# A fifteenth expert input behind the scatter, VectorE's work interleaved block by block there, and 64-wide products in alternation

## What is computed

```python
# first block: retention state of the context, per head (8 heads, keys 64 wide, values 128 wide)
w = jnp.exp(lg[:, None] * (l - 1 - jnp.arange(l)))
s = jnp.einsum('bhld,bhle,hl->bhde', k, v, w)          # one forward, one backward

# second block, RWKV-7 (8 heads of 64)
w_log = -jax.nn.softplus(-(w0 + jnp.tanh(zw) @ w_up)) - 0.5
a = jax.nn.sigmoid(a0 + za @ a_up)
g = jax.nn.sigmoid(zg) @ g_up
# per step: S = S * w_t + (S @ -kk_t) b_t + v_t k_t;  y_t = S @ r_t

# second block, PEER
act = jax.nn.gelu(jnp.einsum('tkd,td->tk', u_emb[eb], tb), approximate=False) * gb
out = jnp.einsum('tk,tkd->td', act, v_emb[eb])
```

## Time and profile before

| | us |
|---|---|
| median of 3 runs | 1875.15 (1874.86 to 1876.91) |
| the profiled execution | 1877.81 |
| its span, first to last instruction | 1876.0 |
| TensorE busy | 1740.2 (93%) |
| VectorE busy | 1184.8 (63%) |
| ScalarE busy | 814.3 (43%) |
| mean granted clock of TensorE | 0.956 |

### The profile page before, as it was taken

How to read it: one execution, slowest core, us unless ns; L and a number is a source line. 1 busy time by engine, 2 the same in 40 slices (tenths; PEclk the granted TensorE clock), 3 DMA queues, 4 the chain that set the end, 5 groups by cost and what they waited for, 6 DMA issues and landing times.

```text
span 1876.0 us, 31040 instructions
## 1 busy us (share of the span) xinstructions
PE 1740.2 (93%) x11808; PEld 1579.8 (84%) x11808; DVE 1184.8 (63%) x2140; ACT 814.3 (43%) x1223; POOL 110.6 (6%) x124
## 2 busy tenths in 40 slices
PE   8799889899998988788889988799999999999997
PEld 1799868899998976687688877699999999999997
DVE  0656556677745657742357999666666666666665
ACT  2334346466544465311241289244444444444443
POOL 0000000022200000150003400000000000000000
PEclk9899899899999989887699999999999999999999
DMA  8576313445553521100133310355555555555553
GB/s 320 210 268 228 111 45 137 177 167 184 183 185 126 187 92 68 68 1 1 68 113 135 131 43 31 135 182 193 185 181 196 182 183 196 180 184 195 180 186 116
DMA packets 38527, 279.13 MB, mean 149 GB/s; under 512 B 4400, under 2 KB 4528, under 8 KB 5040
## 3 DMA queue, kind: packets, MB, share of 16 engines
q1 hardware_dynamic: 35136, 254.82, 38.3%
q0 software_dynamic: 2304, 16.78, 2.3%
q10 hardware_dynamic: 1008, 6.41, 0.9%
HBM read 276.94 MB, written 1.05 MB: 148 GB/s over the span
## 4 chain that ended last, share of the span: by engine, by line
PE 82%; DVE 10%; ACT 4%; issue 2%; DMA 1%; DVEq 0%; SPq 0%; POOL 0%; ACTq 0%; POOLq 0%
PE ps L443 81%; DVE piece L1479 1%; DMA ring<-in_stream 1%; ACT piece L1062 1%; DVE arena L1793 1%; DVE pconst_sb L2126 1%; DVE cols L2126 0%; DVE late L2126 0%; DVE arena L1536 0%; DVE arena L1559 0%; DVE arena L1885 0%; ACT arena L1096 0%; DVEq L2126 0%; DVE late L2143 0%; ACT arena L1166 0%
## 5 line engine op out<-in xcount | busy, mean ns | idle before, releaser
L443 PEld LDWEIGHTS ps<-h_r,piece 128*128 128x128 f32 x5664 | 708.6, 195 | 37.0 <-issue 25.4
L443 PE MATMUL ps<-h_r,piece 128*128 128x256 f32 x5664 | 716.3, 286 | 21.6 <-DVE h_r L1540 9.5
L1479 DVE TENSOR_TENSOR piece<-ring,piece 128x1024 fp32r<-128x1024 f32 x434 | 535.0, 1239 | 307.4 <-ACT piece L1062 305.9
L1062 ACT ACTIVATE piece<-ring 128x1024 fp32r<-128x1024 f32 x432 | 453.3, 1056 | 408.9 <-PE ps L443 395.8
L443 PE MATMUL ps<-piece,late_r 128*128 128x512 f32 x1536 | 374.4, 393 | 9.9 <-DVE late_r L2148 9.9
L443 PEld LDWEIGHTS ps<-piece,late_r 128*128 128x128 f32 x1536 | 282.5, 190 | 66.5 <-issue 10.8
L443 PE MATMUL ps<-arena 64*128 64x256 f32 (+7 forms) x712 | 126.4, 386 | 34.1 <-DVE arena L1826 8.8
L2143 DVE TENSOR_TENSOR late<-late,arena 128x256 f32<-128x256 f32 x114 | 72.7, 638 | 119.6 <-ACT late L1441 119.6
L443 PEld LDWEIGHTS ps<-arena 128*128 128x128 f32 (+3 forms) x712 | 94.9, 210 | 60.6 <-issue 20.5
L1441 ACT ACTIVATE late<-ps 128x256 f32<-128x256 f32 x114 | 43.9, 385 | 202.7 <-PE ps L443 202.7
L443 PE MATMUL ps<-arena,ring 128*128 128x256 f32 x480 | 110.5, 379 | 1.6 <-DVE arena L1536 1.6
(11 more groups left out here) (309 smaller groups left out, 1813.6 us busy)
## 6 DMA issues: line engine op xcount, KB each, us to landing
ring<-in_stream SPq DMA_DIRECT2D x240, 1024.0 KB, 4.9
arena<-in_mod POOLq DMA_DIRECT2D x16, 1024.0 KB, 5.6
arena<-in_const ACTq DMA_DIRECT2D x1, 2256.0 KB, 8.4
arena<-in_const ACTq DMA_DIRECT2D x1, 2000.0 KB, 9.6
xres<-in_xT SPq DMA_DIRECT2D x1, 1024.0 KB, 10.6
arena<-in_xT SPq DMA_DIRECT2D x1, 1024.0 KB, 12.6
arena<-in_subk ACTq DMA_DIRECT2D x1, 1024.0 KB, 4.8
out<-arena SPq DMA_DIRECT2D x2, 512.0 KB, 2.7
```

What stands on the lines that cost most here:

```text
L443: mm_last[0] = nc.tensor.matmul(*args, **kw)
L1062: A(piece[:, 0, c % 3], ring[:, p % RING, s], ACT.Copy).then_inc(S["hi_ready"], 1)
L1479: TT(piece[:, 1, c % 3], ring[:, p % RING, s], piece[:, 0, c % 3].bitcast(F32), ALU.subtract).then_inc(S["lo_ready"], 1)
```

## The change

- **A fifteenth early input.** EARLY is 15. The fifteenth up block is not done in the scatter but right behind it, in the split form, from the first piece of the page that used to hold the first two down pieces; its GELU goes into the tile `early` too. The down blocks that come before the loop are now 13. The rest, 113 pairs, is 18 rounds of 6 in the loop and five pairs written out behind it, on TensorE, ScalarE and VectorE.
- **Banks.** The ups within the scatter go to bank 0 and the scatter's third gate bank is 1; before, it was the other way round.
- **VectorE's order behind the scatter.** Gate chain e, then one low half, then gate chain e + 1, and so on, instead of two low halves and two chains.
- **Products of 64.** State and y products alternate between the two column halves at each product, with the y products of a pair of heads ordered by shape; the lora products alternate between the two row halves. ScalarE takes the lora outputs in the order q = 0, 2, 1, 3, 4, 5, and VectorE and TensorE wait for six of them instead of four.

```diff
 LOOP = 6
-EARLY = 14
+EARLY = 15
 CHOICE = 10
...
          ("wo", 4), ("up", 22), ("dn", 11), ("lora", 1), ("rkv", 6), ("mqk", 4), ("mv", 2), ("mo", 2),
-         ("gt", 8), ("pm", 2), ("pr", 2), ("w2", 4), ("wq", 8), ("early", EARLY // 2), ("first", (EARLY - 2) // 2),
+         ("gt", 8), ("pm", 2), ("pr", 2), ("w2", 4), ("wq", 8), ("early", EARLY // 2), ("first", (EARLY - 1) // 2),
          ("peer", 129 - EARLY)]
...
         row_hot = [v.rearrange("p (n e) -> p n e", n=4) for v in (at(768, 512, late), at(1280, 512, late), row_more, small)]
-        gate_banks = (6, 7, 0)
+        up_bank = (TURN["peer"] + EARLY - 1) % 2
+        gate_banks = (6, 7, 1 - up_bank)
         col_hot = [v.rearrange("p (n e) -> p n e", n=2) for v in (at(1792, 256, late), cols[:, 0:256],
...
             for d, kw in enumerate((kw_f, kw_b)):
-                for hh in range(8):
-                    r, j = (hh % 2) * 64, hh // 2
+                for j in range(4):
                     for tt in range(2):
-                        m = mm(ps[r:r + 64, 2 + d, j * P:(j + 1) * P], kw[:, tt, hh * 64:(hh + 1) * 64],
-                               vc_tok[:, tt, hh * P:(hh + 1) * P], start=tt == 0, stop=tt == 1)
+                        for hh in (2 * j, 2 * j + 1):
+                            r = (hh % 2) * 64
+                            m = mm(ps[r:r + 64, 2 + d, j * P:(j + 1) * P], kw[:, tt, hh * 64:(hh + 1) * 64],
+                                   vc_tok[:, tt, hh * P:(hh + 1) * P], start=tt == 0, stop=tt == 1, skip_group_check=True)
                 m.then_inc(S["state_mm"], 1)
...
             wa_up, g_up = c2("wa_up"), c2("g_up")
-            for q in range(6):
+            for q in (0, 1, 4, 5):
                 for e in range(2):
                     m_ = (2 * q + e) % 4
-                    o = ps[:, 2 + q, e * L:(e + 1) * L]
+                    half = slice(e * L, (e + 1) * L)
                     if q < 2:
-                        m = mm(o, wa_up[0:64, m_ * P:(m_ + 1) * P], lora_in[0:64, 0, :], start=True, stop=True)
-                    elif q < 4:
-                        m = mm(o, wa_up[64:128, m_ * P:(m_ + 1) * P], zs[64:128, 12, :], start=True, stop=True)
+                        m = mm(ps[:, 2 + q, half], wa_up[0:64, m_ * P:(m_ + 1) * P], lora_in[0:64, 0, :], start=True, stop=True)
+                        if e == 1:
+                            m.then_inc(S["lora_mm"], 1)
+                        m = mm(ps[:, 4 + q, half], wa_up[64:128, m_ * P:(m_ + 1) * P], zs[64:128, 12, :], start=True, stop=True)
                     else:
-                        m = mm(o, g_up[:, m_ * P:(m_ + 1) * P], lora_in[:, 1, :], start=True, stop=True)
+                        m = mm(ps[:, 2 + q, half], g_up[:, m_ * P:(m_ + 1) * P], lora_in[:, 1, :], start=True, stop=True)
                 m.then_inc(S["lora_mm"], 1)
...
             pe.wait_ge(S["kk_sq"], 1)
-            pe.wait_ge(S["lora_act"], 4)
+            pe.wait_ge(S["lora_act"], 6)
             for q in range(2):
...
             for i in range(2):
-                for hh in range(8):
-                    r, j, c, n = (hh % 2) * 64, hh // 2, slice(hh * 64, (hh + 1) * 64), 8 * i + hh
-                    o = ps[r:r + 64, 6 + i, j * P:(j + 1) * P]
-                    mm(o, sa[:, i, c], gram[:, n, 1, :], start=True, stop=False)
-                    mm(o, vtok[:, i, c], gram[:, n, 3, :], start=False, stop=False)
+                for j in range(4):
+                    two = [(ps[r:r + 64, 6 + i, j * P:(j + 1) * P], r, slice(2 * j * 64 + r, 2 * j * 64 + r + 64),
+                            8 * i + 2 * j + r // 64) for r in (0, 64)]
+                    for o, r, c, n in two:
+                        mm(o, sa[:, i, c], gram[:, n, 1, :], start=True, stop=False, skip_group_check=True)
+                    for o, r, c, n in two:
+                        mm(o, vtok[:, i, c], gram[:, n, 3, :], start=False, stop=False, skip_group_check=True)
                     for e in range(2):
-                        m = mm(o[:, e * 64:(e + 1) * 64], states[r:r + 64, 2 * i + e, j, :],
-                               ar[r:r + 64, j, i, 1, e * 64:(e + 1) * 64], start=False, stop=e == 1)
+                        for o, r, c, n in two:
+                            m = mm(o[:, e * 64:(e + 1) * 64], states[r:r + 64, 2 * i + e, j, :],
+                                   ar[r:r + 64, j, i, 1, e * 64:(e + 1) * 64], start=False, stop=e == 1,
+                                   skip_group_check=True)
                 m.then_inc(S["y_mm"], 1)
...
                     pe.wait_ge(loaded[p % RING], 16 * (p // RING + 1))
-                m = mm(ps[:, 1, (T % 2) * L:(T % 2 + 1) * L], ring[:, p % RING, e % 2, k, :], h_full[:, k, :], start=k == 0,
+                m = mm(ps[:, up_bank, (T % 2) * L:(T % 2 + 1) * L], ring[:, p % RING, e % 2, k, :], h_full[:, k, :], start=k == 0,
                        stop=k == 7)
...
                 n, k = (q - 3) // 14, (q - 3) % 14
-                if 0 <= n < EARLY - CHOICE and k < 8:
+                if 0 <= n < EARLY - 1 - CHOICE and k < 8:
                     early_step(8 * n + k)
...
+            pe.wait_ge(S["h_new"], 24)
+            turn(T0 + EARLY)
+            up(EARLY - 1, C0)
             pe.wait_ge(S["g_sb"], L // 4)
-            pe.wait_ge(S["h_new"], 24)
             for e in range(EARLY - 2):
-                down(e, C0 + e)
-            with pe.Fori(0, (P - EARLY) // LOOP) as i:
+                down(e, C0 + 1 + e)
+            rounds = (P - EARLY) // LOOP
+            with pe.Fori(0, rounds) as i:
                 for u in range(LOOP):
...
                     up(EARLY + u, C1 + 2 * u + 1, i)
+            for u in range(LOOP * rounds, P - EARLY):
+                down(EARLY - 2 + u, C1 + 2 * u)
+                up(EARLY + u, C1 + 2 * u + 1)
             down(P - 2, C1 + 2 * (P - EARLY))
...
             gate_page(4)
-            for q in range(6):
-                act.wait_ge(S["lora_mm"], q + 1)
+            for n, q in enumerate((0, 2, 1, 3, 4, 5)):
+                act.wait_ge(S["lora_mm"], n + 1)
                 for e in range(2):
...
                     gates_out(q - 2)
-                if late_e < EARLY and q == 13 + 14 * (late_e - CHOICE):
+                if late_e < EARLY - 1 and q == 13 + 14 * (late_e - CHOICE):
                     T = TURN["peer"] + late_e
                     act.wait_ge(S["acc_ready"], T + 1)
-                    A(early[:, late_e, :], ps[:, 1, (T % 2) * L:(T % 2 + 1) * L], ACT.Gelu).then_inc(acc_free[T % 2], 1)
+                    A(early[:, late_e, :], ps[:, up_bank, (T % 2) * L:(T % 2 + 1) * L], ACT.Gelu).then_inc(acc_free[T % 2], 1)
                     late_e += 1
...
             act.wait_ge(S["hi_ready"], piece_no(PAGE["first"]) + 2)
-            for u in range(1, (EARLY - 2) // 2):
+            early_gelu(EARLY - 1)
+            for u in range(1, (EARLY - 1) // 2):
                 split(PAGE["first"] + u)
             split(PAGE["peer"])
-            with act.Fori(0, (P - EARLY) // LOOP) as i:
+            rounds = (P - EARLY) // LOOP
+            with act.Fori(0, rounds) as i:
                 for u in range(LOOP):
...
                     gelu(EARLY + u, i)
+            for u in range(LOOP * rounds, P - EARLY):
+                split(PAGE["peer"] + 1 + u)
+                gelu(EARLY + u)
             act.wait_ge(S["a_ready"], P)
...
+            def low(p, s, i=0):
+
+                c = piece_no(p) + s
+                dve.wait_ge(S["hi_ready"], c + 1 + 2 * LOOP * i)
+                TT(piece[:, 1, c % 3], ring[:, p % RING, s], piece[:, 0, c % 3].bitcast(F32),
+                   ALU.subtract).then_inc(S["lo_ready"], 1)
+
             def split(p, i=0):
...
                 for s in range(2):
-                    c = piece_no(p) + s
-                    dve.wait_ge(S["hi_ready"], c + 1 + 2 * LOOP * i)
-                    TT(piece[:, 1, c % 3], ring[:, p % RING, s], piece[:, 0, c % 3].bitcast(F32),
-                       ALU.subtract).then_inc(S["lo_ready"], 1)
+                    low(p, s, i)
...
             gate_page(4)
-            dve.wait_ge(S["lora_act"], 4)
+            dve.wait_ge(S["lora_act"], 6)
             dv(TS(lw, lw, -EXP_HALF, None, ALU.mult))
...
                 if e >= 2:
-                    dve.wait_ge(S["piece_used"], piece_no(PAGE["first"]) + e)
+                    dve.wait_ge(S["piece_used"], piece_no(PAGE["first"]) + e + 1)
                 gate(e, 0, early[:, e, :])
...
-            early_gate(0)
-            early_gate(1)
-            for e in range(2, EARLY, 2):
-                split(PAGE["first"] + e // 2)
+            for e in range(EARLY - 2):
                 early_gate(e)
-                early_gate(e + 1)
-            with dve.Fori(0, (P - EARLY) // LOOP) as i:
+                if e < EARLY - 3:
+                    low(PAGE["first"] + (e + 2) // 2, (e + 2) % 2)
+            low(PAGE["peer"], 0)
+            early_gate(EARLY - 2)
+            early_gate(EARLY - 1)
```

(6 more changed lines are left out.)

## The result

The changed kernel takes 1847.02 us, the median of 4 runs (1845.52 to 1848.16), beside 1875.01 (1874.86 to 1876.91, 4 runs) for the kernel before on the same chip: a ratio of 0.9848, with a 95% interval of 0.9831 to 0.9865. The gain is 28.0 us; 24.7 were forecast. The time lies within the stated range, 1843 to 1858.5, but outside the forecast's own 1848 to 1853. The profiled execution took 1848.16 with a span of 1846.3, which is 29.7 under the span before. First the page: busy time by engine, and the shares of the chain that ended last.

The account below looks back on a forecast made before the run. TensorE, with 82% of the chain that ended last, was taken to bound the kernel. Gains of 12.1 (early experts) and 13.3 (y) less 0.7 (lora) made 24.7 us: 1850.5 us, own range 1848 to 1853, with rivals 1843 to 1858.5.

Parts of the forecast that it names:

- The early experts: Behind the scatter: up(14) fills TensorE's idle start, down blocks then run at 2.73 without bursts; gain 12.1 us, bounds 8 to 12.5.
- Rival 4: Early blocks: VectorE still sets the pace, five stalls of 1.56 stay, only the start is filled; 1858.3 us, chance 0.08.
- The y products: Second block's y stage: column halves overlap and changes of shape drop to 16, 26.63 us to 13.3; gain 13.3.
- rival 1: The clock rises inside the y products, some 5 us in; 5.8 us more gain, 1844.7 us, chance 0.17.
- an unchanged clock: Y products: the clock was taken to stay at 0.50 (1.2 GHz) through the whole stage of 13.3 us.
- the forecast's prices: Y products at half clock: 0.107 us per overlapped 128-row product, 0.054 per 64-row one, 0.19 per change of shape.
- Rival 2: Y products: the 64-row products don't overlap in one bank; y gain 9.9, time 1853.9 us, chance 0.13.
- Rival 3: Y products: no column halves overlap, only changes of shape go; gain 3.0, time 1860.8 us, chance 0.08.
- Lora: Lora products: VectorE's chain waits for two more ScalarE outputs, 0.71 us; charged as a 0.7 loss, bounds 0 and 0.8.
- State products: State products already run two by two, so alternating them finer gives 0, within 0.2 either way.
- The five rounds written out: Behind the loop: the loop's own work as straight code, costing 0.
- Rival 5: Five rounds written out behind the loop: instruction fetch makes each round grow, so slower; 1880.5 us at 6 us each, chance 0.02.

Follow-up runs that it names:

- e5: Kernel before with the fifteenth early input and the banks, but VectorE's order still in pairs (low halves, then gate chains): 1865.36 us, ratio 0.9947.
- e6: Kernel before with fourteen early inputs and only VectorE's order interleaved (one low half, one gate chain): 1865.97 us, ratio 0.9946.
- e8: Kernel before with alternating y products, per token tile all over 128 rows, then all over 64, so 4 shape runs, not 16: 1855.89 us, ratio 0.9888.
- e7: Kernel before with y products ordered by shape within a pair of heads, but both products of a column half in a row: 1856.09 us, ratio 0.9888.
- e1: Changed kernel with the lora products, ScalarE's order there and the waits put back as before: 1844.08 us, ratio 0.9827.
- e4: Kernel before with only the lora products, ScalarE's order and their waits changed: 1879.98 us, ratio 1.0017.
- e9: Changed kernel keeping TensorE's alternation of the lora products, with ScalarE's order and the waits for four outputs as before: 1843.5 us, ratio 0.9826.
- e10: Changed kernel with TensorE's lora products in the old order, keeping ScalarE's new order and the waits for six: 1843.71 us, ratio 0.9829.
- e2: Kernel before with only the y products in the changed kernel's new order: 1854.1 us, ratio 0.9884.

## Why the prediction was right, and where it was not

**The early experts: right, with the credit in the wrong place.** Forecast 12.1, measured 12.5. Its steps are in the trace: GELU 3.22 after up(14) starts (forecast 3.15), high half 0.28 behind it, down(1) 1162.67 - 1158.38 = 4.29 after down(0), which is 1.56 over the pace of 2.73 (forecast 1.6); down blocks at 2.73 with no wait in between; up(15) 3.04 after down(13), which by that pace starts at 1162.67 + 12 x 2.73 = 1195.43 (forecast 3.15); and no half clock. What the text let a reader think, that the interleaving takes the stalls, is half true: e5 has most of the gain without it, and e6 has it without the fifteenth input. Rival 4 took VectorE's work per block as what could fail; e5 gives VectorE the same work in pairs and has no stalls of 1.56, so the bursts came from the order of its work against the pieces, not from the amount.

**The y products: the overlap right, the clock wrong.** Forecast 13.3, measured 19.8; rival 1, which had 0.17, said 13.3 + 5.8 = 19.1 and is what came true. The step that failed is the choice of an unchanged clock, 0.50 through all 128 products: it was 0.50 for 3.5 us and 1.00 for the 5.8 behind. Its argument, that the 32 products at 873.8 ran side by side at half clock, was weak: they last 1.74, and here the clock rose only after 3.5. The parts of the sum hold while the clock is low. TensorE's weight loads after, grouped between changes of shape:

```profile
887.37 1.34 PEld L444 LDWEIGHTS ps<-arena 64*64 64x64 f32 x16 [0.33 <-issue]
889.05 1.09 PEld L444 LDWEIGHTS ps<-arena 64*64 64x64 f32 x16 [0.33 <-issue]
...
892.24 0.80 PEld L444 LDWEIGHTS ps<-arena 64*64 64x64 f32 x16 [0.17 <-issue]
893.21 0.80 PEld L444 LDWEIGHTS ps<-arena 64*64 64x64 f32 x16 [0.17 <-issue]
```

At half clock one period of 16 instructions and two changes is 889.05 - 887.37 = 1.68. By the forecast's prices it is 8 x 0.107 + 8 x 0.054 + 2 x 0.19 = 1.67. At full clock it is 893.21 - 892.24 = 0.97, not half of that: the products halve to 0.64, which leaves 0.16 for a change, hardly less than 0.19. So the rest after the rise did not halve, and that is why 9.27 was measured and not the 8.4 that 3.5 and half of 9.8 would make. In e8 the twelve changes fewer save 1.54, 0.13 each. That is less than either price. Part of it is that its stretch of half clock is filled with products, which halve when the clock rises, and not with changes, which hardly do; the rest stays open.

**Rival 2** is out by the same row: without overlap of the 64-row products, 16 x 0.107 = 1.71 is more than the 1.68 measured, with the changes still to come. The Trainium skill, "TensorEngine Tiling (Array Packing)", "Restrictions and Gotchas", says that different row tiles cannot access one PSUM bank at the same time. The y products of this case do so, in two different column halves, and e8 shows it at 0.032 each; where the page and these runs differ, the runs decide. **Rival 3** (23 us) is out, and e7 says what was at work: the halves need no alternation, only the same shape next to each other.

**Lora: the sign right, the size off by five.** VectorE's first step now starts 743.38 - 741.05 = 2.33 after ScalarE's first sigmoid, before 743.64 - 742.05 = 1.59: the 0.74 of the forecast's 0.71. The rows after:

```profile
741.05 0.83 ACT L1331 ACTIVATE arena<-ps,cols 128x256 f32<-128x256 f32 x2
```

```profile
743.38 0.69 DVE L1870 TENSOR_SCALAR arena<-arena 128x1024 f32<-128x1024 f32 x1 [1.20 <-ACT arena L1331]
```

I took that for the loss, between bounds of 0 and 0.8. The step that failed is "as if nothing behind it gave it back", read as a worst case: VectorE had 0.4 us to spare ahead of GpSimd, so only 0.31 reached TensorE, and the loss was 3.5 all the same, five times the price, through the clock (e1, e4, e9, e10). TensorE done 0.95 sooner and released 0.31 later both lengthen one wait; I priced the first as worth nothing and the second as a delay, and never added the two as idle time of TensorE.

**State products: 0, as forecast.** 64 instructions take 5.92 before and 5.66 after, but 5.43 in e2 and 5.22 in e6 with the old code there. **The five rounds written out: nothing.** Rival 5 is out: from up(15) to the end it is 1846.3 - 1198.47 = 647.8 in the changed kernel. Before it was 1876.0 - 1228.23 = 647.8 from its up(15).

The forecast of 1850.5 was thus 3.5 too high: 6.5 too little for y, 0.4 too little for the early experts and 1.0 of phase, less 2.8 for lora. By the stages that makes 5.1. The other 1.6 is that the profiled executions differ by 29.65 (1877.81 - 1848.16) and the medians by 28.0. That the time came out only 3.5 from the forecast is partly luck: rival 1 came true in y, 6.5 over the forecast, and 2.8 of lora that no rival had, with the 1.6, took most of that away.

## What to carry to other kernels

When products of half the array's columns are laid out, put those of one shape next to each other for both halves: the order within a shape hardly matters, each change of shape does. Before an engine that waits is made to wait longer, or given its idle time earlier, add up how long TensorE will then stand: two shifts that were free alone took it to 1.2 GHz together, for the work behind. The length of a wait doesn't settle it by itself, so look at the granted clock behind each wait in the trace. And where work comes in bursts, look first for an order that is off by one piece; one extra unit ahead of it may cure as much as rewriting the order.

## What the runs showed of the hardware

- TensorE ran the y products without a pause for 26.63 us at 1.2 GHz; the same products two by two went to 2.4 GHz after 3.5 to 3.9 us in each of the eight kernels that have them so. Being busy was not enough for it.
- Products of two column halves go side by side also when two or four of one half come in a row (e7: 9.37 against 9.28), and also into one bank from different row halves (0.032 each). A change of shape costs 0.19 at half clock and 0.16 at full.
- Of the waits ahead of the gate page, 2.05 and 2.40 left the clock at 2.4 GHz, after 2.57 it was 1.2 for 3.4 us, after 3.31 for 6.8. The length alone doesn't decide. The same wait of 3.06 before the 24 products at 779.67 left it at 2.4 GHz, and one of 3.05 in the changed kernel did not; a wait of 4.62 behind the y stage left it there in e2 and not in e8.
- VectorE's low half took 1.21 us alone and 2.19 where GpSimd worked for its first 1.11.
- Kernels with the same code reach the lora products up to 2.7 us apart (736.95 to 739.68), by the stretches of half clock that they meet. What sets where these fall stays open, and a difference of that size between two kernels says nothing of an edit.
